# Opening of a two-stream transformer layer: where the first scaling, splitting and row copies are done

## The reference

```python
mod = jnp.einsum('bd,de->be', jax.nn.silu(cvec), lp['w_ada']) + lp['b_ada']
sh1, sc1, gt1, sh2, sc2, gt2 = jnp.split(mod[:, None, :], 6, axis=-1)
h = rms_norm(x, lp['norm1_g']) * (1 + sc1) + sh1
proj = h @ lp['w_in']                  # [q | k | v | pool input | gate_a | gate_b]
# then attention, a pooling mixer, a gated merge, w_out, a mixture of 16 experts, a last norm
```

## Time and profile before

| | |
|---|---|
| median of 3 runs | 1575.13 us (1573.92 to 1576.98) |
| the profiled execution | 1573.45 us, of which 1571.7 us is the span of its instructions |
| TensorE busy | 1478.0 us, 94% of the span |
| VectorE, ScalarE, GpSimd busy | 1006.7, 655.5, 324.7 us |
| mean granted TensorE clock | 0.973 of full speed |

### The profile page before, as it was taken

The page is one execution under the profiler, slowest core; times in us unless marked ns, Lnnn a source line. Parts: engine busy times, 40 slices in busy tenths (PEclk is TensorE's granted clock), DMA queues, the critical chain, the costliest instruction groups (busy, mean ns, idle before and its releaser), DMA issues.

```text
span 1571.7 us, 22081 instructions
## 1 busy us (share of the span) xinstructions
PE 1478.0 (94%) x8155; PEld 1233.6 (78%) x8155; DVE 1006.7 (64%) x1505; ACT 655.5 (42%) x889; POOL 324.7 (21%) x229
## 2 busy tenths in 40 slices
PE   5999999999999899999999999999999699999990
PEld 4788888777888678888788888888888588888870
DVE  7698433046546477778777764334457788888775
ACT  6312222221123555666565642111232376667653
POOL 0111111123324101101100000000000156766540
PEclk9999999999999999999999999999999699999995
DMA  9345443320001010001000024424424468888857
GB/s 375 133 158 183 163 162 146 109 99 28 28 30 65 34 44 1 0 0 44 1 0 0 34 96 164 136 80 137 178 81 188 140 221 258 269 261 241 246 141 286
DMA packets 52449, 194.81 MB, mean 124 GB/s; under 512 B 9371, under 2 KB 18443, under 8 KB 40993
## 3 DMA queue, kind: packets, MB, share of 16 engines
q1 hardware_dynamic: 42144, 172.31, 30.5%
q0 software_dynamic: 10240, 21.61, 6.1%
HBM read 157.03 MB, written 43.58 MB: 128 GB/s over the span
## 4 chain that ended last, share of the span: by engine, by line
PE 44%; DVE 9%; ACT 5%; DMA 4%; issue 3%; POOL 1%; DVEq 0%; POOLq 0%; SPq 0%; ACTq 0%
PE psum L1636 9%; PE psum L1816 4%; PE psum L1592 4%; PE psum L1837 4%; PE psum L1741 4%; PE psum L1820 2%; PE psum L1578 2%; PE psum L1575 2%; PE psum L1576 2%; PE psum L1752 2%; DMA xg<-h2d,x_row 2%; PE psum L1561 2%; PE psum L1563 2%; PE psum L1562 2%; ACT prob L1902 2%
## 5 line engine op out<-in xcount | busy, mean ns | idle before, releaser
L353 PE MATMUL psum<-h_hi,w_hi 128*128 128x512 f32 x720 | 182.9, 362 | 2.1 <-issue 2.1
L353 PE MATMUL psum<-h_lo,w_hi 128*128 128x512 f32 x720 | 179.7, 358 | 0.0
L353 PE MATMUL psum<-h_hi,w_lo 128*128 128x512 f32 x720 | 179.4, 357 | 0.0
L2145 DVE TENSOR_TENSOR pT_lo<-psum,pT_hi 128x512 fp32r<-128x512 f32 x192 | 126.3, 686 | 55.3 <-ACT pT_hi L1908 55.3
L353 PEld LDWEIGHTS psum<-h_hi,w_hi 128*128 128x128 f32 x720 | 119.8, 188 | 28.7 <-issue 8.5
L709 POOL TENSOR_TENSOR w_lo<-w_raw,w_hi 128x1024 fp32r<-128x1024 f32 x30 | 74.6, 2486 | 321.9 <-ACT w_hi L555 321.9
L1908 ACT CAST pT_hi<-psum 128x512 fp32r<-128x512 f32 x192 | 104.6, 588 | 84.4 <-PE psum L1592 84.1
L353 PEld LDWEIGHTS psum<-h_lo,w_hi 128*128 128x128 f32 x720 | 119.5, 188 | 21.6 <-issue 0.5
L353 PEld LDWEIGHTS psum<-h_hi,w_lo 128*128 128x128 f32 x720 | 119.4, 188 | 21.3
L864 DVE SCALAR_TENSOR_TENSOR ada_junk<-adaT,cs_rows 128x1024 f32<-128x1024 f32 x64 | 85.8, 1340 | 69.1 <-DMA adaT<-in_w_adaT 66.3
L1902 ACT ACTIVATE prob<-psum,nmax,q_row 128x1536 f32<-128x1536 f32 x64 | 104.6, 1634 | 31.6 <-DVE nmax L2139 31.5
(11 more groups left out here) (387 smaller groups left out, 3013.2 us busy)
## 6 DMA issues: line engine op xcount, KB each, us to landing
gu_raw<-in_w_gu SPq DMA_DIRECT2D x32, 1024.0 KB, 6.8
w_raw<-in_w_in SPq DMA_DIRECT2D x16, 1024.0 KB, 4.8
adaT<-in_w_adaT SPq DMA_DIRECT2D x16, 1024.0 KB, 6.1
dn_raw<-in_w_dn SPq DMA_DIRECT2D x16, 1024.0 KB, 8.4
gates<-gst SPq DMA_DIRECT2D x14, 640.0 KB, 3.1
xt<-in_x SPq DMA_DIRECT2D x10, 512.0 KB, 8.1
merged<-gates SPq DMA_DIRECT2D x8, 640.0 KB, 3.9
stage<-gates SPq DMA_DIRECT2D x8, 640.0 KB, 4.0
```

Of the source, the lines that this page charges most:

```text
L353: mm = pe.matmul(psum[:, par_sets[j] + g:par_sets[j] + g + w], a[j][:, k, :], b[:, k, g:g + w], start=(k == 0 and a is w_hi and b is h_hi) ...
L2145: nc.vector.tensor_tensor(pT_lo[b][g % 2][:], psum[:, TP + 512 * b:TP + 512 * b + 512], pT_hi[b][g % 2][:], ALU.subtract).then_inc(s[f"a_t ...
```

## The change

Four edits, all in the first 40 us:

- Tiles 1, 3, 5 and 7 are multiplied by their factor on GpSimd instead of VectorE (`X_POOL`). VectorE raises a new semaphore `x_root` once the factors of a pair stand, and GpSimd a new `x_scaled_p` per tile. Tile 9 stays on VectorE.
- The low parts of the first pair of weights are made on GpSimd behind these four (`split(n, j)` from n = 0), and `first_split` goes.
- The rows of blocks 0 and 1 are copied out of PSUM by ScalarE, between its halves of turned tiles. Those of blocks 2 to 7 stay on VectorE.
- TensorE does `first_turn(0)` and `first_ada(1)` ahead of the turn of tile 9, and VectorE does `first_mods(0)` ahead of its half of tile 9.

```diff
+        X_POOL = (1, 3, 5, 7)
@@ TensorE, turn_x
-                    pe.wait_ge(s["x_scaled"], t + 1)
+                    if t in X_POOL:
+                        pe.wait_ge(s["x_scaled_p"], X_POOL.index(t) + 1)
+                    else:
+                        pe.wait_ge(s["x_scaled"], t + 1 - sum(u < t for u in X_POOL))
@@ TensorE
                 first_ada(0)
                 turn_x(TILES - 2)
-                turn_x(TILES - 1)
                 first_turn(0)
                 first_ada(1)
+                turn_x(TILES - 1)
                 first_turn(1)
@@ ScalarE
+                def first_rows(i):
+                    act.wait_ge(s["fa_mm"], i + 1)
+                    nc.scalar.copy(ada_rows[i][:], psum[:, ROWS_AT:ROWS_AT + PAIR]).then_inc(s["fa_rows"], 1)
                 act_out(TILES - 4)
+                first_rows(0)
                 act_out(TILES - 3)
                 split(0, 0)
                 act_out(TILES - 2)
+                first_rows(1)
                 act_out(TILES - 1)
                 split(0, 1)
@@ GpSimd
-                for n in range(1, G0 + 1):
+                for i, u in enumerate(X_POOL):
+                    pool.wait_ge(s["x_root"], u // 2 + 1)
+                    nc.gpsimd.tensor_scalar(xt[:, u, :], xt[:, u, :], rstd[:, u:u + 1], None, ALU.mult).then_inc(s["x_scaled_p"], 1)
+                for n in range(0, G0 + 1):
@@ VectorE
                     inverse(rstd[:, h], nsq[:, h], ntmp[:, h])
+                    dve.sem_inc(s["x_root"], 1)
                     for u in (t, t + 1):
-                        nc.vector.tensor_scalar(xt[:, u, :], xt[:, u, :], rstd[:, u:u + 1], None, ALU.mult).then_inc(s["x_scaled"], 1)
+                        if u not in X_POOL:
+                            nc.vector.tensor_scalar(xt[:, u, :], xt[:, u, :], rstd[:, u:u + 1], None, ALU.mult).then_inc(s["x_scaled"], 1)
                         if t:
                             dve_out(u - 2)
-                first_rows(0)
                 dve_out(TILES - 2)
+                first_mods(0)
                 dve_out(TILES - 1)
-                first_mods(0)
-                first_split(0)
-                first_rows(1)
                 first_mods(1)
@@ VectorE, in the loop over pairs of parts
                     low(k + 1)
-                    if k == 0:
-                        first_split(1)
```

More of the change, by code:

```diff
@@ L173, in build @@
         s = {}
-        for n in ("eps_r x_ss csq_r csd_st csd_in rs_used consts rope wpool_in icnt_in x_sq x_scaled xT_ps xT_outa xT_outd c_in c_sig c_silu fa_mm fa_rows fa_turn fa_mods ada_mm0 ada_mm1 ada_in0 ada_in1 "
+        for n in ("eps_r x_ss x_root x_scaled_p csq_r csd_st csd_in rs_used consts rope wpool_in icnt_in x_sq x_scaled xT_ps xT_outa xT_outd c_in c_sig c_silu fa_mm fa_rows fa_turn fa_mods ada_mm0 ada_mm1 ada_in0 ada_in1 "
                   "mods_b h_raw h_hi_r h_lo_r w_in0 w_hi0 w_hi1 w_lo0 w_lo1 mm0 mm1 ps_free0 ps_free1 pad0 xp_in xp_used "
@@ L815, in low @@
                     nc.vector.tensor_tensor(h_lo[:, k, :], h_full[:, k, :], h_hi[:, k, :], ALU.subtract).then_inc(s["h_lo_r"], 1)
-                def first_split(j):
-                    dve.wait_ge(s[f"w_hi{j}"], 1)
-                    nc.vector.tensor_tensor(w_lo[j][:], w_raw[:, :, j * P:(j + 1) * P], w_hi[j][:], ALU.subtract).then_inc(s[f"w_lo{j}"], 1)
                 for t in range(0, TILES, 2):
```

## The result

The changed kernel takes 1579.31 us (median of 20 runs, 1575.12 to 1584.6) against 1574.31 us of the kernel before (median of 20 runs). The ratio is 1.003 with a 95% interval of 1.002 to 1.0039. It is slower by about 4.7 us (0.003 x 1574); forecast was 0.5 us faster, and a range that ended at 1577.5. One of the 20 runs of the kernel before took 2982.71 us and is left out of the ratio.

A forecast was written before the change was run, and what follows sets the result against it. TensorE, 94% busy, was taken as the bound, so only an earlier start of its unbroken stretch counts: 2.3 lead - 1.5 VectorE behind GpSimd - 0.3 clock = 0.5 us, median 1574.6 us, 8-in-10 range 1571.2 to 1577.5.

The forecast's parts named there:

- What bounds it: Opening: TensorE's waits before its unbroken stretch from 33.61 us; the change is worth only what it moves there.
- The price of a scaling on GpSimd: x tiles: 1.2 us per scaling, taken as one-input work, between a cast-based 1.2 and a two-input 2.49 us.
- the third rival: x tiles: scaling costs as much as two inputs, 2.4 us, holding up VectorE's small steps; 1576.1 us, chance 0.15.
- VectorE behind GpSimd's second low part: First chunk: `h_full` waits for GpSimd until 32.15, TensorE waits about 0.8 us for `h_lo`; takes 1.5 us off the lead.
- The clock: First chunks: low clock of 1.2 GHz ends at the same moment, 39.4 us, costing 0.3 us of the lead.
- The sum: Whole kernel: 2.3 - 1.5 - 0.3 = 0.5 us faster, with ends of 0 and 1 us.
- GpSimd gets in first: x tiles: GpSimd's scaling starts first, VectorE's stands behind it 1.2 us in each of four pairs; 1577.0, chance 0.13.

The follow-up runs named there:

- changed again: The changed kernel timed and profiled a second time, with no edit; ratio 1.0031 to the kernel before.
- changed without low parts: Changed kernel with both low parts of the first pair of weights back on VectorE, GpSimd still scaling four tiles; ratio 1.0003 to the kernel before.
- changed without scaling: Changed kernel with all tiles scaled on VectorE, the other three edits kept; ratio 1.0025 to the kernel before.
- one low part on GpSimd: Changed kernel with all scalings and the second low part back on VectorE, only the first low part on GpSimd; ratio 0.9988 to the kernel before.
- The added transposes: Changed kernel with identity transposes on TensorE in its three opening waits (12, 12 and 6), into unread PSUM; ratio 1.0012 to the kernel before.
- low parts alone: Kernel before with only the second edit, both low parts of the first pair of weights on GpSimd; ratio 1.0006 to the kernel before.
- rows and order alone: Changed kernel without its first two edits: all scalings and both low parts on VectorE; ratio 0.9997 to the kernel before.

## Why the prediction was wrong

**What bounds it** held as far as the runs show: the opening changed by what TensorE waited for and by the clock over the work behind it, and nothing later is seen to follow the change.

**The price of a scaling on GpSimd** is the first step that failed. I took 1.2 us between ends of 1.2 and 2.49; it is 2.84 by itself, above both ends, and 2.6 behind VectorE's. So the bound from above, the two-input subtraction of the same size, was no bound, and one-input work has no one price on GpSimd: against VectorE's 0.75 us for the same scaling, the rule cited in the prediction, roughly line-rate for one input, does not hold here. The case that came is the third rival, which had 0.15: its 0.4 and 0.8 us of held-up small instructions are 0.44 to 0.58 per pair in the trace. It had tile 7 at 24.1, though, and the rows of block 2 one microsecond late; they were 1.98 us late. My forecast of tile 8 at 22.9 became 25.81, and that of the first product, 31.3, became 34.35. Without the scaling it was 32.09, 1.5 us ahead of before where I had 2.3, and with it 2.26 us later.

These 2.26 us have two parts. 1.36 us stand at tile 8's scaling (25.81 against 24.45), and that moment scatters: 24.19 to 25.81 us in the four profiles that have edits three and four and GpSimd's scaling, 24.45 to 25.35 in the four that have these edits without it. The other 0.90 us is steady: from tile 8's scaling to the first product it is 8.54 us in "changed", "changed again" and "changed without low parts", and 7.64 and 7.63 us in "changed without scaling" and "one low part on GpSimd". It is tile 7, which I had turned at 22.15 and which was turned at 25.50, when GpSimd let it go, with block 0's product and tile 8 behind it.

**VectorE behind GpSimd's second low part** was right in place and mechanism. The one-input form of VectorE is held too: `h_full` took 3.19 us, and the Trainium skill's page "SBUF — State Buffer" (section "Who interferes with whom"), which has the one-input fast form contend as well, agrees with this row. It also has the engine that starts first keep the ports for its whole instruction, and there the trace differs: L775, with two inputs in SBUF, passed at 20.77, in the middle of GpSimd's scaling (18.32 to 21.70). TensorE's wait was 1.55 us where I had 0.8. The hold-up itself was sized well: from the start of `h_hi` to the end of `h_lo` I had 5.05 us, and it took 4.76. What was not is the work ahead of the wait, the two groups of products from the first one on. A wait of 0.8 us up to 34.5 leaves them 2.4 us from 31.3, about what they took before at 1.2 GHz (2.27 us, 33.61 to 35.88); in the changed kernel they took 1.39 us at 2.4 GHz. In the kernel without the scaling, where the clock fell at 32.5 over this very work, the wait was 0.83 us.

**The clock** is the second step that failed, and the dearer one as far as the ratios tell. I let it come back at the same moment, at a cost of 0.3 us; it came back 6.1 us later (45.5 against 39.4), and the cost was 1.5. Set against the distance without any low clock and without the hold-up (38.93), the changed kernel has 43.31 = 38.93 + 1.55 + 2.83, and the kernel before 40.23 = 38.93 + 1.30. Before, part of the low stretch covered work that would have waited for VectorE anyway; after, it fell behind the hold-up, over unbroken work. The added transposes took away those 2.83 us in the changed kernel's profile, and nothing else of it, and by the ratios 2.8 to 3.0 us. That the hold-up alone moves the low stretch isn't shown: in "low parts alone" it also lay late, without a wait for `h_lo`.

**The sum** at the landmark, measured in place of forecast: first product +0.74 (scaling +2.26, the other edits -1.52), hold-up +1.55, clock +1.53 (2.83 - 1.30), together 3.82 = 77.66 - 73.84. These are single profiles.

**Which of the two edits weighs more** is better read from the ratios. With the low parts back on VectorE, 1.003 becomes 1.0003, a gain of 4.2 us and clear of the scatter. With the scaling back on VectorE it becomes 1.0025, a gain of 0.8 us that can't be told from none; alone, the scaling costs 2.5 us. The second low part by itself stands between "changed without scaling" (1.0025) and "one low part on GpSimd" (0.9988): 5.8 us, and clear of the scatter. So most of the loss is the second low part on GpSimd with the low clock behind it, not the dear scaling.

The rival "GpSimd gets in first" did not come: both scalings of a pair start together (10.51 and 10.51, 22.06 and 22.06), and VectorE's takes 0.75 us, undisturbed. Only that of the second pair (13.32, 1.13 us) stood behind GpSimd's scaling of the first, to 13.89.

**What stays open.** The ratio is worth 4.7 us, the opening 3.8 and 2.1 us in the two profiles. In the first, another 3.2 us arose far later: the last product with `wo_hi` and `mh` (L1746) starts 128.8 us after the first, 125.6 us before, with the granted clock at 0.73 and 0.59 between 1115 and 1125 us. That stretch took 128.7 us in the profile of the kernel before with transposes added too, 127.1 in the second profile of the changed kernel, 125.6 in that of the changed kernel without the scaling, and 127.1 to 128.8 in all the others, so it doesn't follow the change. Whether a late opening makes it more frequent wasn't tried. Also open is why tile 8's scaling waited 0.58 us for its factors in the kernels with `X_POOL = ()`.

## What to carry to other kernels

An operation moved to an idle engine has to be timed there by itself: on GpSimd the row of a copy says nothing of a scaling by a factor per partition. Check what the receiving engine's instruction holds up: behind GpSimd's work from SBUF, VectorE's smallest instruction can stand for its whole rest (1.34 us instead of 0.17), and the next engine may be waiting for just that one. Ahead of a long unbroken stretch of TensorE, a new wait can cost more than its length, because the clock may then be low over the work behind it (here 1.55 us of wait and 1.5 us of clock). So move work off VectorE where its next instructions read PSUM, and not where they are one-input instructions on SBUF. The first low part is of the one kind: on GpSimd it held nothing up and won 0.25 us between tile 8's scaling and the first product (7.63 against 7.88), though the ratios (0.9988 and 0.9997) don't tell the two apart. The second is of the other.

## What the runs showed of the hardware

- GpSimd, 128 x 1024 float32, by itself: scaling by a per-partition factor 2.84 us, copy 1.04, memset 0.98 each; 128 x 512 scaling 1.57.
- What GpSimd's scaling holds up hangs on the form of VectorE's instruction and on its moment. In the five profiles that have these scalings (3.38 us each, 3.26 where one follows another), every one-input TENSOR_SCALAR of VectorE that began 2.41 us or more after GpSimd's start stood until GpSimd's end, 20 of them, down to 128 x 2. Those that began at its start or 1.41 to 2.32 us after it, 36 of them, passed. TENSOR_TENSORs with two inputs in SBUF and RECIPROCALs passed always, as late as 2.88 us.
- GpSimd's subtraction holds VectorE's one-input instructions earlier: L805 in "low parts alone" was held from 29.96 to 31.30, from about 1.0 us behind the start of the second of two that end at 31.28 (4.68 us in all). VectorE's copies out of PSUM ran beside it at their usual length (0.69 us at 31.02).
- The low clock in the opening differs between executions of near-identical kernels: none (rows and order alone), 38.7 to 45.5 (changed), 35.6 to 42.4 (changed again), 33.9 to 37.3 (changed without low parts), 32.5 to 42.7 (changed without scaling). A single profile is no measure of it; the ratios are.
